# x's second quarter is turned between the second and third k tile of the first block

## What is computed

```
def reference(x, mem, positions, norm_mix, w_in, ...):
    for layer in range(DEPTH):
        h = rms_norm(x, norm_mix[layer])
        x = x + token_mixer(h, cos, sin, w_in[layer], ...)
        x = x + memory_cross_attention(rms_norm(x, ...), rms_norm(mem, ...), ...)
        h = rms_norm(x, norm_ffn[layer])
        x = x + (swiglu(h, ...) if layer % 2 == 0 else moe_ffn(h, ...))
    return rms_norm(x, norm_final)
```

## Time and profile before

| | us |
|---|---|
| median of 3 runs | 1994.55 |
| their range | 1994.39 to 1995.96 |
| the profiled execution | 1995.11 |
| its span | 1992.9 |
| TensorE busy in it | 1973.7 |
| VectorE, ScalarE busy | 1508.8, 1263.3 |

### The profile page before, as it was taken

One profiled execution on the slowest core, in us unless ns is written; L12 is line 12 of the kernel. 1 busy time (PEld: TensorE's weight loads), 2 busy tenths in 40 slices (PEclk: granted clock), 3 DMA queues, 4 the chain that ended last, 5 costly groups with the idle time before them and its releaser, 6 DMA issues.

```text
span 1992.9 us, 25117 instructions
## 1 busy us (share of the span) xinstructions
PE 1973.7 (99%) x9258; PEld 1632.3 (82%) x9258; DVE 1508.8 (76%) x1394; ACT 1263.3 (63%) x1251; POOL 112.8 (6%) x166
## 2 busy tenths in 40 slices
PE   8999999999999999999999999999999999999998
PEld 7887888888888887788887888888888888888886
DVE  6877665555556777765459988889888988988998
ACT  6566545453434456645556776777777777776776
POOL 4300000000000210000000000100000000000130
PEclk9999999999999999999989999999999999999999
DMA  8445655455555554665369999999999999999994
GB/s 287 164 153 148 180 181 169 140 183 189 186 189 179 169 161 152 168 230 188 127 235 341 401 390 379 385 374 377 387 375 400 359 389 383 366 392 381 384 401 185
DMA packets 195497, 539.58 MB, mean 271 GB/s; under 512 B 10264, under 2 KB 18016, under 8 KB 195424
## 3 DMA queue, kind: packets, MB, share of 16 engines
q1 hardware_dynamic: 192592, 529.65, 73.6%
q0 software_dynamic: 2448, 8.91, 1.2%
q10 hardware_dynamic: 384, 0.03, 0.0%
HBM read 530.17 MB, written 8.39 MB: 270 GB/s over the span
## 4 chain that ended last, share of the span: by engine, by line
PE 94%; DVE 3%; issue 1%; SPq 1%; ACT 1%; DMA 0%; DVEq 0%; ACTq 0%
PE bank L2518 14%; PE bank L2520 14%; PE bank L2519 14%; PE bank L2102 14%; PE bank L2104 14%; PE bank L2103 14%; PE bank L2150 2%; PE bank L2587 1%; DVE expert_lo L1338 1%; PE bank L2273 1%; PE bank L2291 1%; SPq L590 1%; PE bank L2168 1%; PE bank L2190 1%; DMA raw<-in_w_in 0%
## 5 line engine op out<-in xcount | busy, mean ns | idle before, releaser
L843 ACT ACTIVATE w_hi<-raw 128x2048 fp32r<-128x2048 f32 x341 | 638.1, 1922 | 122.3 <-DMA raw<-in_moe_w_gu 81.2
L1338 DVE TENSOR_TENSOR expert_lo<-raw,w_hi 128x2048 fp32r<-128x2048 f32 x284 | 639.3, 2295 | 27.4 <-ACT w_hi L843 27.3
L2518 PE MATMUL bank<-w_hi,stat 128*128 128x512 f32 x1312 | 515.3, 393 | 1.5 <-DVE expert_lo L1338 1.4
L2520 PE MATMUL bank<-w_hi,stat 128*128 128x512 f32 x1312 | 511.7, 390 | 0.0
L2102 PE MATMUL bank<-w_hi,stat 128*128 128x512 f32 (+1 forms) x1296 | 511.3, 394 | 0.0
L2104 PE MATMUL bank<-w_hi,stat 128*128 128x512 f32 (+1 forms) x1296 | 503.6, 389 | 0.0
L1319 DVE TENSOR_TENSOR low_in_place<-raw,w_hi 128x2048 fp32r<-128x2048 f32 (+1 forms) x161 | 367.7, 2285 | 179.3 <-ACT w_hi L837 179.1
L2103 PE MATMUL bank<-low_in_place,stat 128*128 128x512 f32 (+1 forms) x1296 | 503.3, 388 | 0.0
L2519 PE MATMUL bank<-expert_lo,stat 128*128 128x512 f32 x1088 | 423.8, 390 | 0.0
L837 ACT ACTIVATE w_hi<-raw 128x2048 fp32r<-128x2048 f32 (+1 forms) x161 | 305.7, 1903 | 179.7 <-DMA raw<-in_dense_w_gu 61.7
L2518 PEld LDWEIGHTS bank<-w_hi,stat 128*128 128x128 f32 x1312 | 246.4, 188 | 52.0 <-DVE expert_lo L1338 2.3
(11 more groups left out here) (314 smaller groups left out, 1234.2 us busy)
## 6 DMA issues: line engine op xcount, KB each, us to landing
raw<-in_moe_w_gu SPq DMA_DIRECT2D x224, 1024.0 KB, 7.7
raw<-in_moe_w_down SPq DMA_DIRECT2D x112, 1024.0 KB, 8.4
raw<-in_w_in SPq DMA_DIRECT2D x55, 1024.0 KB, 5.0
raw<-in_dense_w_gu SPq DMA_DIRECT2D x28, 1024.0 KB, 5.1
raw<-in_w_xkv SPq DMA_DIRECT2D x16, 1024.0 KB, 5.2
raw<-in_dense_w_down SPq DMA_DIRECT2D x14, 1024.0 KB, 5.0
raw<-in_w_branch SPq DMA_DIRECT2D x8, 1024.0 KB, 5.1
raw<-in_w_branch SPq DMA_DIRECT2D x16, 512.0 KB, 6.3
```

The lines of the kernel that those rows point to most:

```text
L843: act.activation(expert_hi(b), expert_raw(b), ACT.Copy).then_inc(hi_done, 1)
L1338: dve.tensor_tensor(expert_low(b), expert_raw(b), f32_of(expert_hi(b)), ALU.subtract).then_inc(lo_done, 1)
L2518: pe.matmul(dst[:, :], x_hi, wh[:, at], start=start, stop=False)
L2520: ins = pe.matmul(dst[:, :], x_lo, wh[:, at], start=False, stop=stop)
```

## The change

The four transposes of x's second quarter (h1), and the wait for its load, are taken from ahead of the first product. They now stand in `opening_piece`, ahead of the waits of the third k tile. Nothing else is edited.

```diff
             def opening_piece(kt):
 
+                if kt == 2:
+                    pe.wait_ge(x_landed[1], 16)
+                    rows_t(0, "h1", x, 1)
                 if kt % 2 == 0:
                     emptied(0, f"h{kt // 2}")
...
-            for q in range(2):
-                pe.wait_ge(x_landed[q], 16)
-                rows_t(0, f"h{q}", x, q)
+            pe.wait_ge(x_landed[0], 16)
+            rows_t(0, "h0", x, 0)
```

## The result

The changed kernel takes 2000.27 us in the median of 15 runs (1999.30 to 2000.99), and the kernel before takes 1994.88 (15 runs, 1994.39 to 1996.07). The ratio is 1.0025, with a 95% interval of 1.0018 to 1.0033, so the change is slower by about 5.4 us (3.6 to 6.6 by that interval). The profiled execution took 1999.36 us for a span of 1997.1. Beside the one of before (1995.11 for 1992.9) that is 4.25 us more, against a forecast of 4.15. The forecast against the median was 1998.7, and is 1.6 us too low, though still inside the interval. The range of 1996.3 to 2000.3 holds the median only just.

What follows compares the result with a forecast made beforehand. TensorE was taken to bound the kernel. First product 0, opening delay 4.8 and 0.67 given back sum to +4.15 us, which on the median of 1994.55 gives 1998.7 us, range 1996.3 to 2000.3.

Steps and rivals of the forecast that it cites:

- The first product: Opening: it still starts at 8.16 us, held by VectorE's low half of the weights; gain taken as 0.
- Its price for the four transposes: Ahead of the first product: 0.95 us at the low clock, the gain if nothing else held that product.
- The chain behind h1: From h1's transposes at 10.86 through ScalarE and VectorE to the third k tile's product at 14.51: 3.65 us.
- The clock: Behind the gap, from 14.51 us: low clock until near 17.8, making the opening's delay 4.8 us; chance 0.50.
- The rival of a clock that stays high: Behind the gap: clock rises at about 11.5 and holds; delay 2.3 us, 1996.9 us in all; chance 0.27.
- the reading by the row: Opening clock: choice and sum went by trace rows alone, not by the skill's sentence that transposes do not bring full clock.
- What is given back: TensorE's three waits at 45.09, 51.23 and 51.95 us vanish: 0.67 us regained, bounds 0.49 and 1.02.
- The rival of an absorbed delay: Until 52 us: the chain from the load landing at 30.28 sets the pace; 1994.6 us, chance 0.08.
- The rest of the run, a term taken as zero: Behind 52 us: every listed wait depends on TensorE itself, so no further slack was found.
- the prediction's own sign: From 60 us to the end: the prediction is wrong if the shift changes there.
- a longer low clock in the opening: Behind the gap: clock rises only at 19.4 us; delay 4.9 us, 1999.5 us in all; chance 0.13.

Runs made afterwards that it cites:

- e5: Kernel before with thirteen identity transposes added in TensorE's waits ahead of the first product, results unused; median 1994.90 us, ratio 0.9999.
- e9: Kernel before with fourteen transposes added in TensorE's waits at the router of the second layer; median 1994.93 us, ratio 0.9997.
- e1: Changed kernel with h1's four transposes one k tile earlier, between the first and second k tile; median 1998.67 us, ratio 1.0015.
- e3: Changed kernel with fourteen more 128-column transposes behind h1's, in TensorE's gap, results unused; median 1997.82 us, ratio 1.0015.
- e10: Changed kernel run again unedited for a second profile; profiled execution 1999.15 us.
- e11: Changed kernel run again unedited for a third profile; profiled execution 2000.93 us.
- e2: Changed kernel with eight more 512-column products behind h1's transposes, in TensorE's gap, results unused; median 1998.06 us, ratio 1.0016.
- e4: Changed kernel with ScalarE's and VectorE's work on the weights of k tiles 2 and 3 ahead of their work on h1; median 1999.12 us, ratio 1.0019.
- e6: Changed kernel with seventeen transposes added ahead of the first product and twenty behind h1's, in TensorE's opening waits; median 1996.60 us, ratio 1.0007.
- e7: Kernel before with twelve more 512-column products between the first block's two token tiles, results unused; median 1996.99 us, ratio 1.0010.
- e8: Kernel before with thirteen transposes added ahead of the first product and fourteen at the second layer's router; median 1994.71 us, ratio 0.9997.

## Why the prediction was right or wrong

**The first product: right for the landing of x in the trace.** It stays at 8.16, bounded by VectorE's low half. e5 shows the bound directly, with 0.47 us of waiting behind transposes that were long through. Where x's second quarter came at 8.03 (e9), the transposes were the bound, and the prediction named no such case. Its price for the four transposes, 0.95 us from 7.21 to 8.16, holds that wait too: from their start to the product it is 0.76 in e9, where nothing else was waited for. Eight took 1.56 at the low clock, so 0.20 each and not 0.24.

**The chain behind h1: right.** The forecast of 3.65 us was put together from the trace of before. It measures 3.59 here, 3.58, 3.53 and 3.50 in e1 to e3. The third tile's product was forecast at 14.51 and came at 14.44.

**The clock: right in size, wrong in form.** The forecast was a low clock from 14.5 on, "not yet risen at the gap rather than lost in it". In all three profiles of the changed kernel it had risen and was then lost, near 15.6 in the first, at the same product in e10, and near 14.5 in e11. A delay of 4.8 us was forecast, and 4.96, 4.78 and 4.85 were measured at 20 us. e2 and e3 separate the term: 1.7 us of it is the low clock (forecast 4.8 - 3.0 = 1.8). That the size came out with another course of the clock is in part luck. The rival of a clock that stays high came true only where TensorE was kept busy, and in the one profile of e1, with a gap of 1.25 us; neither is in the change. What decides between a clock that is kept, lost or not yet risen (e4) is open.

**The transposes: the reading by the row holds.** By the sentence from the Trainium skill, "TensorE: Matmul & The Clock Gate", Part 4, transposes would not hold the clock. In e3, fourteen transposes held it as well as eight products did in e2, and in e5 they raised it. The trace lists them as MATMUL with `ident` and doesn't say in which mode they ran; the kernel calls `pe.transpose`. Here the measurement differs from the page, and it decides.

**What is given back: right.** 0.67 was forecast within 0.49 to 1.02, and 0.81 was measured (0.74 to 0.82 in e1 to e4, e6, e7, e10 and e11). All three waits of the earlier trace rows are gone. The 0.67 does not follow from its own terms: 0.49 and the 0.53 less 0.2 to 0.3 are 0.72 to 0.82, which is what was measured. The rival of an absorbed delay fell with e7: 2.06 us were still there at the router.

**The rest of the run, a term taken as zero: the step that failed.** "Behind 52 us every entry in the list of waits depends on TensorE itself" is right for the waits, but the speed of TensorE at the router isn't the same in each execution. The sum of 4.15 us holds between two profiled executions that both have a router stage of 16.39 us (4.25 measured). Against the medians it is 5.4. The profiled execution of the change is 0.91 below its median, and that of before 0.23 above its own. That makes up the difference of 1.1 us. In the three profiles it doesn't come from the opening: they have 4.15, 3.98 and 4.11 at the router. The one with 2000.93 us has its excess in the router stage, where the low clock lasted longer. By the prediction's own sign, a shift that changes between 60 us and the end, that execution contradicts it: 4.1 us at the router, 5.8 at the end. Of the 15 timed runs, ten are at 2000.10 or above and five at 1999.30 to 1999.59. The profiles of 1999.15 and 1999.36 are like the five. No run between 2000.1 and 2000.5 was profiled, so it is an inference that the median's excess lies in the router stage too. If it does, the changed kernel comes upon the longer stage more often than the kernel before, and why is open. Both reach the router with the same work behind them, and differ by 4 us in when.

**The chances.** 0.59 went to a change within 0.2% and 0.39 to slower. The median is 0.25% above, on the side that was given less. The forecast stood on that line, and all its uncertainty was put inside the opening. The trace of before had shown the low clock at the router. A term of its own for it, with its sign unknown, would have been due, and the weight of the slower side with it, since the delay behind which it comes was 4.15 already. The upper end of the range, 2000.3, carried the median with 0.03 to spare. That is luck: it was set for a longer low clock in the opening, not for the router.

## What to carry over

Work that leaves the shadow of a wait is only free if nothing stands behind it. Here four transposes of under 1 us cost 3.3 us, because the steps of two other engines that hang on them lost their cover of six products. Write down the chain from the moved instruction to the next one that needs it, and add the distances in the trace; that gave the place of the third tile's product to within 0.1 us. And look at the clock of TensorE twice, behind the gap that a change opens and at each later stage of light work: such a stage differed by 1.6 us between executions of one kernel here, and lay between 15.70 and 18.03 us over all kernels that leave it as it is, so one profile doesn't carry a forecast of a few us against a median.

## What the runs showed of the hardware

- Transposes of 128x128 in f32 raised the clock by themselves: with 5 and 8 of them in the waits ahead of the first product, the products were 0.23 us apart from 8.47 on (e5), and 0.43 without them. In e8 the same thirteen were followed by a wait of 0.44 us for x, and the products were 0.24 us apart only from 9.21 on.
- A high clock can be lost behind a gap that is already over. It fell near 15.6 us, 1.1 us after the products had come back at 14.44, and came back near 19.0, under work without a break.
- A shorter gap isn't always the better one. Behind 0.95, 1.06 and 1.25 us (e2, e3, e1) the clock was high, behind 1.84 (e4) it was low until about 19.4 us, behind 2.53 it was lost for a part. In e4 no row shows that the clock had risen before the gap ended, so the length of the gap alone isn't shown to be the cause.
- The same kernel's router stage took 16.39, 16.40 and 18.03 us in three executions, with the same waits. What differs is how long the clock is low: e11 is at 0.50 from 1022 to 1034 throughout, e10 is back at 0.86 in the last two of these.
- The granted clock column reads 1.00 in the first microseconds while the products are 0.43 us apart. Later it agrees with them (0.51 from 15.5 to 18.5 us).
